# A four-branch mixer encoder step: the next tile's triangular head placed between two averages, and cumulated decays loaded instead of summed on TensorE

## What is computed

```
h = rms_norm(x, g_pre);  p = h @ w_in              # 51 tiles of 128 channels, and 8 dt columns
ya = rg_lru(conv(xa)) * silu(ga)                   # branch a
yb = rwkv7_mix(pb) * silu(gb)                      # branch b: inverse of a triangular 64x64 matrix per head and chunk
yc = rms_norm(ssd_scan(conv(xbc), dt) * silu(z))   # branch c: decays exp(acs_t - acs_s), acs = cumsum(dt * A)
yd = rms_norm(hgrn2(qd, fd, id)) * silu(gd)        # branch d: gated linear attention
x  = x + rms_norm(concat(ya, yb, yc, yd) @ w_out)
x  = x + rms_norm(cross_attn(rms_norm(x), mem_k, mem_v))
```

## Time and profile before

| | |
|---|---|
| time, median of 3 runs | 3781.03 us (3768.44 to 3786.89) |
| the profiled execution's own time | 3779.5 us |
| span of its profile | 3777.7 us |
| granted TensorE clock, mean over the span | 0.932 |
| busy: PE, DVE, ACT, POOL | 3241.9, 1600.5, 913.2, 314.0 us |
| DMA | 325.21 MB, mean 86 GB/s |

### The profile page before, as it was taken

The page is one execution under the profiler, slowest core; times in us unless marked ns, Lnnn a source line. Parts: engine busy times, 40 slices in busy tenths (PEclk is TensorE's granted clock), DMA queues, the critical chain, the costliest instruction groups (busy, mean ns, idle before and its releaser), DMA issues. The chain is left out here.

```text
span 3777.7 us, 72832 instructions
## 1 busy us (share of the span) xinstructions
PE 3241.9 (86%) x30816; PEld 2811.6 (74%) x30816; DVE 1600.5 (42%) x2516; ACT 913.2 (24%) x1767; POOL 314.0 (8%) x402
## 2 busy tenths in 40 slices
PE   3899999999999988867787777777757699969998
PEld 2799999999999975556676766666644388858887
DVE  5476555565244422334344434434421332234443
ACT  2276544432122210012221221222210211121111
POOL 4000000000000000121211211211220000000000
PEclk9999999999999989978888888989976899989999
DMA  4011222222552253332322322232233143341221
GB/s 104 16 45 43 95 91 88 92 88 71 64 93 91 93 207 139 136 88 67 93 54 54 84 76 54 74 86 54 62 104 125 42 133 115 113 170 51 67 67 56
DMA packets 401267, 325.21 MB, mean 86 GB/s; under 512 B 92560, under 2 KB 367249, under 8 KB 399985
## 3 DMA queue, kind: packets, MB, share of 16 engines
q1 hardware_dynamic: 374272, 304.16, 27.4%
q0 software_dynamic: 4608, 16.78, 1.1%
q10 hardware_dynamic: 22128, 0.35, 0.3%
HBM read 192.77 MB, written 128.48 MB: 85 GB/s over the span
## 5 line engine op out<-in xcount | busy, mean ns | idle before, releaser
L1114 PE MATMUL in_ps<-in_hT_high,in_w_high 128*128 128x420 f32 x2080 | 751.3, 361 | 9.1 <-DVEq L802 9.1
L1114 PE MATMUL in_ps<-in_hT_high,in_w_low 128*128 128x420 f32 x2080 | 735.6, 354 | 0.0
L1114 PE MATMUL in_ps<-in_hT_low,in_w_high 128*128 128x420 f32 x2080 | 735.1, 353 | 0.0
L1114 PEld LDWEIGHTS in_ps<-in_hT_high,in_w_high 128*128 128x128 f32 x2080 | 392.0, 188 | 33.4 <-issue 27.6
L1114 PEld LDWEIGHTS in_ps<-in_hT_low,in_w_high 128*128 128x128 f32 x2080 | 391.6, 188 | 12.7 <-issue 6.3
L1114 PEld LDWEIGHTS in_ps<-in_hT_high,in_w_low 128*128 128x128 f32 x2080 | 391.8, 188 | 6.7
L2136 DVE TENSOR_TENSOR mixp_qi<-mixp_ps,mixp_eye 128x256 f32<-128x256 f32 x160 | 67.9, 425 | 288.0 <-PE mixp_ps L1808 286.6
L1708 ACT ACTIVATE mixp_tu_inv<-mixp_ps 128x512 f32<-128x512 f32 (+1 forms) x160 | 88.7, 554 | 377.6 <-PE mixp_ps L1808 376.2
L2947 PE MATMUL mixo_ps<-mixo_w_high,mixo_y_high 128*128 128x512 f32 x512 | 158.7, 392 | 18.3 <-DVE mixo_w_low L2923 18.3
L1808 PE MATMUL mixp_ps<-mixp_triu,mixp_dt_in 128*64 128x128 f32 (+1 forms) x512 | 74.8, 349 | 104.3 <-DMA mixp_dt_in<-dts 104.3
L2947 PE MATMUL mixo_ps<-mixo_w_high,mixo_y_low 128*128 128x512 f32 x512 | 158.7, 391 | 0.0
(11 more groups left out here) (592 smaller groups left out, 6022.2 us busy)
## 6 DMA issues: line engine op xcount, KB each, us to landing
pc<-in_outs SPq DMA_DIRECT2D x270, 208.0 KB, 2.0
in_w_tile<-in_w_in_dram SPq DMA_DIRECT2D x52, 512.0 KB, 4.1
mixp_rw_in<-pc SPq DMA_DIRECT2D x16, 1024.0 KB, 6.4
mixo_y_in<-yt SPq DMA_DIRECT2D x16, 1024.0 KB, 6.1
mixp_gate_io<-pc SPq DMA_DIRECT2D x48, 256.0 KB, 3.3
mixp_hg_in<-pc SPq DMA_DIRECT2D x16, 768.0 KB, 6.8
yt<-mixp_gate_io SPq DMA_DIRECT2D x16, 768.0 KB, 5.4
pc<-in_full SPq DMA_DIRECT2D x8, 1040.0 KB, 6.1
```

The costliest lines, as they stand in the source:

```text
L1114: last = pe.matmul(o, left(a, k), right(b, k), start=p is passes[0], stop=p is passes[-1])
```

## The change

It has two parts, both in the mixer passes, and what the second needs in the projection.

1. **The head moves to the tile before.** `mt` and `n_off` of tile i+1 are issued by PE right after `y_rwkv` of tile i, ahead of `yd_ms`; the first half level `q2` between `yb_mean` and `yb_var`; `nt` after `yb_var`. DVE does `mt_pt`, `t_off`, `t0` before `yb_centred`, and `qi2`, `nt_qt` after it; POOL does `lev2`, `u_off`, `u0` between its gains of yd and yb, and `lev4` to `lev32` after. A body now starts with `tu2`. `keys`, `bonus`, `h_att`, `h_keys` are spread between the levels, and `att` on DVE moves behind `qi8`. The averages get other PSUM banks; `yd_ln` and `yd_rms` come ahead of `yb_square`. DVE's `front_yc` moves from between `wkv0` and the copy of `rhs1` to the second chunk (`front_inter` after the `rhs1` copy, the rest after the `sa1` copy). `front_ssd` on ACT moves from before to after the copies of level 16, and DVE's `seg` and scores both stand between `qi16` and `qi32`.
2. **acs comes by DMA.** The projection transposes `acs` (17 small transposes on PE in 5 batches, 5 copies on DVE, one store) into a scratch tensor `acs_t` with tokens along rows. `load_in` loads it for each tile into `acs_in`, 8 rows of 128 floats on each of the 128 partitions; `dt_in` moves to `load_in` too. `sums` and `head_sums` go; `seg`, `e_acs`, `tot` and `d_last` read `acs_in`. SP issues `load_in` after PE's `y_rwkv` and DVE's `wkv1`, no longer after DVE's last step.

```diff
             def load_in(i, j):
...
+                sync.dma_start(dt_in[j][:, :, :], dts[bass.ds(i * TT, TT), :, :]).then_inc(in_loaded[j], 16)
+                rows_of = acs_t[:, :, bass.ds(i * TT + t_first, TT)].broadcast_to([P, HEADS, TT])
+                sync.dma_start(acs_in[j][:, :, :], rows_of).then_inc(in_loaded[j], 16)
...
             def tile(i, j, more):
                 at_tile(i)
-                sync.wait_ge(*v_s.at("y_rwkv"))
-                settle()
                 if more:
                     sync.wait_ge(*pe_s.at("y_rwkv"))
+                    sync.wait_ge(*v_s.at(f"wkv{NCH - 1}"))
                     settle()
                     load_in(i + 2, j)
+                sync.wait_ge(*v_s.at("y_rwkv"))
                 sync.wait_ge(*v_f.before())
...
+                pe.wait_ge(*g_f.at(f"u0{rows[-1].start}", 1))
+                pe.wait_ge(*v_f.at("nt_qt", 1))
+                pe.wait_ge(*a_s.before())
+                settle()
+                tu_level(2)
...
+                tu_level(8)
                 if more:
-                    ready(pe, jn, nn)
                     in_ready(pe, jn, nn)
-                    front_sums(jn, True)
-                q_level(8)
-                if more:
-                    front_head_sums(jn, True)
-                tu_level(8)
+                    front_cb(jn, True)
                 q_level(16)
-                if more:
-                    front_cb(jn)
                 tu_level(16)
...
+                if more:
+                    head_scores(jn)
                 pe.wait_ge(*a_s.at("yd_copy"))
-                pe.wait_ge(*v_s.at(f"wkv{NCH - 1}"))
                 settle()
-                mm(ps[:, 1, 0:4 * TT], c["headmean"][:, :], flat(yd2))
+                mm(ps[:, 7, 0:4 * TT], c["headmean"][:, :], flat(yd2)).then_inc(*pe_s.did("yd_ms"))
                 pe.wait_ge(*a_s.at("yb_copy"))
                 settle()
-                mm(ps[:, 6, 0:4 * TT], c["headmean"][:, :], flat(yb)).then_inc(*pe_s.did("yb_mean"))
+                mm(ps[:, 2, 0:4 * TT], c["headmean"][:, :], flat(yb)).then_inc(*pe_s.did("yb_mean"))
+                if more:
+                    pe.wait_ge(*a_s.at("yd_ln"))
+                    head_level()
                 pe.wait_ge(*a_s.at("yb_square"))
                 settle()
                 mm(ps[:, 2, 0:4 * TT], c["headmean"][:, :], flat(yb2)).then_inc(*pe_s.did("yb_var"))
+                if more:
+                    head_nt(jn)
...
-                qi_level(4)
-                qi_level(8)
+                qi_level(16)
                 if more:
                     in_ready(vec, jn, nn)
-                    ready(vec, jn, nn)
                     front_seg(jn)
-                qi_level(16)
-                if more:
                     front_scores(jn)
                 if L > 32:
                     qi_level(32)
```

More of the change, by code:

```diff
@@ L1143, in sum_dt, with turn_acs @@
                           start=True, stop=True).then_inc(dt_summed, 1)
+            def turn_acs(b):
+                pe.wait_ge(dt_copied, 1)
+                at_least(pe, acs_copied, b)
+                first, end = ACS_BATCHES[b]
+                for t in range(first, end):
+                    r = P if t < NT else TS
+                    last = pe.transpose(ps[0:HEADS, 7, (t - first) * P:(t - first) * P + r], dt_out[0:r, t, 2, :], ident[0:r, 0:r])
+                last.then_inc(acs_turned, 1)
             def rwkv_up(m):
@@ L1255 @@
-            'yc_intra', 'yc_sum', 'yc', 'ssd_decay0', 'ssd_decay1', 'ssd_state', 'y_ssd',
+            'seg', 'seg_clamped', 'd_last', 'cb', 'd_last_dt', 'ssd_scores0', 'ssd_scores1', 'x_dt', 'x_dd',
+            'd_x', 'yc_inter', 'yc_intra', 'yc_sum', 'yc', 'ssd_decay0', 'ssd_decay1', 'ssd_state', 'mt_pt_0',
+            'mt_pt', 't_off0', 't_off64', 't0_0', 't0', 'qi2_0_0', 'qi2_0_64', 'nt_qt_0', 'nt_qt', 'y_ssd',
         ],
         'scalar_front': [
-            'e_acs', 'seg_exp', 'tot0', 'tot1', 'd_last_exp', 'b_tok', 'yc_square', 'yc_ln', 'yc_rms',
+            'seg_exp', 'e_acs0', 'e_acs1', 'tot', 'd_last_exp', 'b_tok', 'yc_square', 'yc_ln', 'yc_rms',
@@ L1430, in mixer_pass @@
         dt_in = [sb(f"dt_in{j}", [TT, 3, HEADS]) for j in range(NB)]
+        acs_in = [sb(f"acs_in{j}", [P, HEADS, TT]) for j in range(NB)]
         kvec = sb("kvec", [P, 6, 4])
@@ L1762, in body @@
                 level(2)
+                act.wait_ge(*pe_s.at("keys"))
+                for r in rows:
+                    b(v_tok[r].rearrange("p c q v -> p (c q v)"), ps[r, 3, 0:NCH * 256], ACT.Copy, f"v_tok{r.start}")
+                    b(k_key[r].rearrange("p c q v -> p (c q v)"), ps[r, 5, 0:NCH * 256], ACT.Copy, f"k_key{r.start}")
+                level(4)
                 act.wait_ge(*pe_s.at("h_keys"))
@@ L1830, in _, with front_cb @@
             pe.wait_ge(states_set, 1)
[L1833 removed]
+            def front_cb(j, prev):
                 if prev:
                     pe.wait_ge(*v_s.at("att"))
[L1837 to L1856 removed]
                 settle()
@@ new lines, in head_scores, with head_level @@
+            def head_scores(j):
+                pe.wait_ge(*v_f.at("ssd_state"))
+                settle()
+                scores(5, bneg[j], j).then_inc(*pe_f.did("mt"))
+                by_head(4, lambda hh, q, k: chunk(kr[j][halves[hh], q, 0, :], k), chan(bneg[j]), L).then_inc(*pe_f.did("n_off"))
+            def head_level():
+                pe.wait_ge(*g_f.at(f"lev2_{rows[-1].start}"))
+                pe.wait_ge(*v_f.at("t0"))
+                settle()
+                for k in range(NCH):
+                    of_chunk(6, 0, lev[2], tinv, k).then_inc(*pe_f.did(f"q2_{k}"))
@@ L1926, in body, with head_nt @@
+            def head_nt(j):
+                pe.wait_ge(*a_f.at("yc_ln"))
+                settle()
+                scores(0, khat[j], j).then_inc(*pe_f.did("nt"))
             def body(j, n, more):
                 jn, nn = next_of(j, n)
[L1929 to L1937 removed]
@@ L1949, in body @@
-                by_head(5, chan(khat[j]), eye, HEAD).then_inc(*pe_s.did("keys"))
-                pe.wait_ge(*v_s.at(f"t_off{rows[-1].start}"))
-                settle()
-                mm(ps[:, 0, 0:4 * TT], c["headones"][:, :], flat(rk[j])).then_inc(*pe_s.did("bonus"))
-                def of_chunk(bank, at, left, right, k):
-                    for h in range(HEADS):
-                        hh, q = h % 2, h // 2
-                        last = mm(ps[hrows[hh], bank + k, at + q * L:at + (q + 1) * L],
-                                  left[hrows[hh], k, q, :], right[hrows[hh], k, q, :])
-                    return last
@@ L2320, in body @@
                             hgrn_states(0)
+                        if more and k == NCH - 1:
+                            if stage == "rhs":
+                                front_inter()
+                            else:
+                                front_yc(jn, nn)
                     vec.wait_ge(*pe_s.at(f"kv{k}"))
```

326 lines of the change are left out of this document (169 added, 157 removed), and 15 rows, old and new, of the table STEPS.

## The result

The changed kernel takes **3648.2 us** (median of 4 runs, 3642.68 to 3651.01) against 3778.3 us for the kernel before in the same comparison: ratio 0.9655, 95% interval 0.9628 to 0.9682. Forecast were 3621 us, in a range of 3575 to 3690. The profiled execution took 3648.3 us, 131 us less than that of before, where the sum had 158.5. Run once more on another occasion it took 3652.2 us, ratio 0.9664 (0.9648 to 0.9680).

A forecast was written before the change was run, and what follows sets the result against it. The prediction took the bound to be a chain hopping between engines once per body, with PE on most of it. Gains and losses 73.3 + 69.6 + 34 + 24.6 - 41 - 4 + 2 = 158.5 us, from 3779.5, gave 3621 us, range 3575 to 3690.

The forecast's parts named there:

- The wait for dt_in: PE's wait for dt_in in the middle of the body goes, as load_in starts about 11 us earlier: gain 73.3 us.
- third rival: PE's wait moves to acs_in, if its broadcast lands as late as dt_in did: 73.3 us stay, 3694 us; chance 8%.
- The sums: Both kinds of sums on PE go: gain 69.6 us over 15 bodies.
- The head: Around the averages, waits for lev, ACT's square and ACT's last step go; new nt_qt wait loses 11: gain 34 us.
- yc: With the yc chain behind the copy of rhs1, PE's wait for rhs shrinks by 1.6 us, 15 times: gain 24.6 us.
- seg between qi16 and qi32: With seg, exponentials and scores all there, PE stands 2.7 us before tu32, 15 times: loss 41 us.
- Small ends: 17 transposes in the projection lose 4 us, the first front changes nothing, the sample's pass gains 2 us.
- the first rival: The clock stays up at the start of a body, 15 times 1.7 us: 3595 us; chance 15%.
- The second rival: DVE's products and POOL's masks take turns at the tile's end, costing 36 us: 3657 us; chance 15%.

The follow-up runs named there:

- late loads: The changed kernel with load_in for tile i+2 issued after DVE's last step of tile i, as before: 3684.5 us, ratio 0.9752.
- the second part alone: The kernel before with acs stored as rows and loaded by DMA, and no sums, everything else where it stood: 3746.9 us, ratio 0.9915.
- the second profile: The same changed kernel, unedited, profiled again: PE busy 550.4 us in eleven bodies, against 557.2.

## Why the prediction was right, and where it was off

The sign, the class and the range held, and the forecast was 27 us too low. By its own steps:

1. **The wait for dt_in**: gone, and no DMA ends a wait at `cb`. `acs_in` landed 8.2 to 10.0 us after its issue, well inside the lead. With late loads the third rival's wait did come, at 31.2 us.
2. **The sums**: gone. But "73.3 + 69.6" as gains that can be counted whole is what the second part alone refutes. Without the rest of the change they came to 32 us.
3. **The head**: `lev` and the wait between the averages went as forecast. The step that failed is the sentence "that time stands under 'issue', and stays". Together with step 1, which issues the loads 11 us earlier, the stands at the jumps went from about 3 us to between 5.5 and 9.8: "issue" plus 32, and 11 under `lev`. `nt_qt` cost 17.1 us for 11.
4. **yc**: as forecast against the kernel before, where the wait for `rhs` fell from 33.6 to 9.2 us, by 24.4. But put back into the changed kernel the chain costs 63.5 us. The wait was 2.2 us in the kernel before, but 3.15 with the chain put back and 3.13 with the second part alone, where PE comes earlier; and the clock was left out.
5. **seg between qi16 and qi32**: the stand was 2.93 us for a forecast of 2.7. Taking it away gained 62 us, not 41, since the clock behind it counts too.
6. **Small ends**: the prompt's mixer starts 1.9 us later, for a forecast of 4, and from the first products of the sample's mixer to the end it is 4.1 us less, for a forecast of 2.

So two terms were missing. The late instructions cost 43 us, 32 under "issue" and 11 under `lev`. The clock gave some of it back: PE needed 557.2 us for what took 570.6 before, 18 us over fifteen bodies, and 550.4 or 28 us in the second profile, around the 26 us that the first rival had for it; it was a rival and should have been a term. With 6 us more for `nt_qt` and 4 us better small ends, 158.5 - 43 - 6 + 18 + 4 gives 131.5, for 131 measured; with the second profile's clock it would be 10 us more, so so close a sum is in part luck.

The second rival's mechanism is in the trace. DVE in order of time at a tile's end:

```profile
2283.99 1.32 DVE L2164 TENSOR_TENSOR mixp_yb<-mixp_yb 128x512 f32<-128x512 f32 x1
2285.23 1.75 DVE L2164 TENSOR_TENSOR mixp_yd<-mixp_yd 128x512 f32<-128x512 f32 x1
2287.01 1.63 DVE L2164 TENSOR_TENSOR mixp_yb<-mixp_yb,mixp_bv 128x512 f32<-128x512 f32 x1
2288.57 0.68 DVE L2170 SCALAR_TENSOR_TENSOR mixp_gate_io<-mixp_yd,mixp_gate_io 128x512 f32<-128x512 f32 x1
```

The first three lie beside POOL's masks (2282.16 to 2288.10) and take up to 1.75 us, the next one alone 0.68. They lose 2.7 us a body, and POOL loses too (5.94 us for four masks, 5.3 by the earlier trace rows). But PE's waits for `qi` outside `tu32` come to 1.9 us in all, so it was hidden, by the slack that the prediction gave as 1.5 us and, at the jumps, by the stands. No run took POOL's masks away, so a small cost is not excluded.

Taking back single parts of the change against the changed kernel gave 36 (early loads) and 63.5 us (yc) of gain and 62 of loss (seg). With the 32 of the second part alone, the move of the head is what is left: 130 - 32 - 36 - 63.5 + 62, about 60 us. It was not tried alone, and since the parts share the late instructions and the clock, this is an account and not a measurement.

## What to carry to other kernels

A long wait may be the cover under which an engine's next instructions arrive; before you count its removal in full, look at what else is on its way to PE at that time: in the profile the stands called "issue" (or named after an event long past) with the DMA share inside them. Count a stand on PE at its own length plus the slow matmuls behind it: here 1.45 us on top of 2.93. If loads run where a loop jumps back, write the loop out (48 us here); moving them away from the jump cost 36 us, since they then met other blocks of instructions.

## What was not expected of the hardware

- PE's instructions come in blocks of 16 KB on a DMA queue, and late while data transfers run: at the stands of the changed kernel the block's packet took 0.9 to 1.9 us, but started up to 6.6 us into the stand. At the same branch PE stood for 2.9 to 3.5 us with next to no transfers and for up to 9.8 us (10.3 in another kernel) with the DMA engines half busy; in the middle of straight code it stood for 4.5 to 6.0 us at a DMA share of 0.7 to 0.8.
- Two useless products of 0.94 us each in a stand of 2.9 us made the kernel 16.5 us faster, twice.
- The broadcast of 512 KB in 1024 rows of 512 bytes landed in 8.8 us (median), between the two that the prediction had as bounds.
